# Steps of a context stream placed among 512 row gathers by the length of their products

## The reference, cut to what matters

```
def _peer(h, w_q, sub_keys, u_tab, v_tab):          # first block
    qry = (t @ w_q) ...;  scores = einsum("thpd,hpkd->thpk", qry, sub_keys)
    s_top, i_top = top_k(scores, 16);  ...;  best, pos = top_k(cand, 16)
    gate = softmax(best)
    u = u_tab[ib];  act = gelu(einsum("td,thkd->thk", tb, u))
    vv = v_tab[ib];  return einsum("thk,thkd->td", gb * act, vv)

# second block, layer 0, the context's part
hc = modulate(rmsnorm(ctx));  ctx = ctx + cg1 * pool_mixer(hc)
ctx = ctx + cg2 * conv_ffn(modulate(rmsnorm(ctx)))   # 1024 -> 2 x 2816 -> 1024, width-3 conv
# layer 1: hc = modulate(rmsnorm(ctx)); keys and values of attention from hc
```

## Time and profile before

| | us |
|---|---|
| median of 3 runs | 1712.83 (1711.22 to 1714.83) |
| the profiled execution, its own time | 1713.59 |
| its span, first to last instruction | 1711.7 |
| first gather issued | 326.9 |
| last gather issued | 1125.3 |

### The profile page before, as it was taken

One profiled execution on the slowest core, in us unless ns is written; L12 is line 12 of the kernel. 1 busy time (PEld: TensorE's weight loads), 2 busy tenths in 40 slices (PEclk: granted clock), 3 DMA queues, 4 the chain that ended last, 5 costly groups with the idle time before them and its releaser, 6 DMA issues.

```text
span 1711.7 us, 23479 instructions
## 1 busy us (share of the span) xinstructions
PE 1498.0 (88%) x9034; PEld 1109.4 (65%) x9034; DVE 1093.5 (64%) x2121; ACT 554.4 (32%) x782; POOL 790.4 (46%) x746
## 2 busy tenths in 40 slices
PE   7999998775566699999788866989999999999999
PEld 6997676663212266666333432449999985699999
DVE  4865654689489867766856665237775436567753
ACT  6652121211221131322100011236654524466542
POOL 0024230276667765746777777624561101225630
PEclk9999999997878899999999997999999898999999
DMA  7447770498999999999999999985654425746550
GB/s 273 149 148 294 278 278 25 158 398 305 384 398 400 409 396 391 394 382 400 406 404 400 404 371 408 408 307 187 195 185 158 175 105 191 266 130 196 192 178 26
DMA packets 188575, 477.24 MB, mean 279 GB/s; under 512 B 10544, under 2 KB 80432, under 8 KB 185264
## 3 DMA queue, kind: packets, MB, share of 16 engines
q0 software_dynamic: 73728, 268.47, 40.3%
q1 hardware_dynamic: 114736, 207.27, 34.1%
HBM read 474.65 MB, written 1.05 MB: 278 GB/s over the span
## 4 chain that ended last, share of the span: by engine, by line
PE 57%; DMA 15%; DVE 10%; POOL 7%; issue 4%; ACT 1%; DVEq 0%; ACTq 0%; SPq 0%; POOLq 0%
PE ps L666 57%; DMA arena<-in_peer_v,cl 8%; POOL arena L2723 6%; DMA wring<-in_ffn_w_up 3%; DVE arena L1802 2%; DMA wring<-in_peer_v,cl 2%; DVE arena L1419 1%; POOL wring L2723 1%; DMA arena<-in_peer_u,arena 1%; PE ps L670 1%; DVE arena L1425 1%; DMA wring<-in_peer_u,arena 1%; DVE wring L1802 1%; DVE arena L1732 0%; DMA wring<-in_ada 0%
## 5 line engine op out<-in xcount | busy, mean ns | idle before, releaser
L666 PE MATMUL ps<-arena,wring 128*128 128x256 f32 (+2 forms) x2360 | 595.5, 489 | 105.5 <-DMA arena<-in_peer_v,cl 97.4
L666 PEld LDWEIGHTS ps<-arena,wring 128*128 128x128 f32 (+1 forms) x2360 | 330.4, 167 | 352.7 <-DMA arena<-in_peer_v,cl 176.5
L1802 DVE CUSTOM_DVE_ANT_0 arena<-arena 128x1024 f32<-128x1024 f32 x214 | 257.2, 1227 | 124.7 <-DMA arena<-in_peer_u,arena 121.3
L2723 POOL DMA_INDIRECT arena<-in_peer_u,arena x214 | 240.2, 1123 | 198.5 <-DVE arena L1760 80.0
L2723 POOL DMA_INDIRECT arena<-in_peer_v,cl x214 | 222.9, 1042 | 82.4 <-issue 57.9
L2130 ACT ACT_TABLE_LOAD x64 | 82.1, 1283 | 388.1 <-DVE arena L1802 266.9
L1419 DVE TENSOR_TENSOR wl<-wring,wh 128x2048 fp32r<-128x2048 f32 (+1 forms) x76 | 167.8, 2208 | 60.7 <-ACT wh L2133 58.6
L666 PE MATMUL ps<-hh,wh 128*128 128x256 f32 x704 | 201.2, 286 | 3.9 <-DVE hl L1425 3.9
L666 PE MATMUL ps<-hl,wh 128*128 128x256 f32 x704 | 200.8, 285 | 0.0
L666 PE MATMUL ps<-hh,wl 128*128 128x256 f32 x704 | 200.7, 285 | 0.0
L1425 DVE SCALAR_TENSOR_TENSOR cvb<-ps,vec,cvb 128x255 f32<-128x255 f32 x264 | 127.5, 483 | 106.9 <-ACT cvb L2130 99.6
(11 more groups left out here) (261 smaller groups left out, 2324.0 us busy)
## 6 DMA issues: line engine op xcount, KB each, us to landing
wring<-in_ffn_w_up SPq DMA_DIRECT2D x66, 1024.0 KB, 8.3
wring<-in_ada SPq DMA_DIRECT2D x24, 2048.0 KB, 8.7
wring<-in_ffn_w_down SPq DMA_DIRECT2D x12, 2048.0 KB, 8.4
wring<-in_w_in SPq DMA_DIRECT2D x8, 2048.0 KB, 8.1
wring<-in_ffn_w_down SPq DMA_DIRECT2D x6, 1536.0 KB, 7.9
wring<-in_peer_wq SPq DMA_DIRECT2D x4, 2048.0 KB, 20.7
wring<-in_attn_w_qkv SPq DMA_DIRECT2D x4, 2048.0 KB, 9.0
wring<-in_w_out SPq DMA_DIRECT2D x2, 2048.0 KB, 8.2
```

Of the source, the lines that this page charges most:

```text
L666: return pe.matmul(o, l, r, start=start, stop=stop)
L1802: ve.tensor_tensor_reduce(out=o, in0=o, in1=h2[:, t, :], scale=1.0, scalar=0.0, op0=MUL, op1=ADD, accum_out=dots[j % 2][:, k:k + 1]).then_ ...
L2723: po.indirect_dma_start(out=ring[n % NR], out_offset=None, in_=table, in_offset=bass.IndirectOffsetOnAxis(ap=which, axis=0)).then_inc(S[f" ...
```

## The change

`woven` no longer compares with an even threshold. It keeps `due`, the rest at which the next step is taken, first 4, and after step k adds `rests(k)`: 4 up to step 9; then 7 after a query product and 2 after its scores up to step 15; 2 for the short and empty steps, but 4 after steps 23 to 26; 10 after each up product (34 to 55); 5 after each down step (58 to 81); 4 from step 89. All three engines use it. The steps' contents, the gathers and the loads' order are the same. The steps stand at these rests, worked out from both rules:

| step | before | after |
|---|---|---|
| 0 to 10 | 4 to 44 | 4 to 44 |
| 12, 14, 15 | 55, 66, 72 | 53, 62, 69 |
| 16 | 77 | 71 |
| 18, 20 | 88, 100 | 75, 79 |
| 22, 26 | 111, 133 | 83, 97 |
| 34 | 178 | 115 |
| 55 | 296 | 325 |
| 58 | 312 | 339 |
| 81 | 441 | 454 |
| 89, 91 | 486, 497 | 473, 481 |

```diff
+    def rests(k):
+
+
+        if k < 10:
+            return 4
+        if k < 16:
+            return 2 if k % 2 else 7
+        return 4 if 23 <= k < 27 or k >= 89 else 10 if 34 <= k < 56 else 5 if 58 <= k < 82 else 2
+
     def woven(peer, context):
 
 
-        n, steps, half = 0, 0, None
+        n, steps, half, due = 0, 0, None, 4
         for what in peer:
             if what == "rest":
                 n += 1
                 if n == half:
                     next(context, None)
                     half = None
-                elif n >= (4 * (steps + 1) if steps < 11 else 44 + 56 * (steps - 10) // 10):
+                elif n >= due:
+                    due += rests(steps)
                     steps += 1
                     if next(context, None) == "half":
                         half = n + 3
```

## The result

The changed kernel took 1718.57 us in the median of 20 runs against 1714.84 us for the kernel before in as many; the ratio is 1.0023 with an interval of 1.0014 to 1.0032. A repetition with 12 runs gave 1716.08 us and a ratio of 1.0004 (0.9992 to 1.0016). So it is no faster: +0.23% or 3.7 us in the first comparison, whose interval leaves out zero, and +0.04% in the second, whose interval includes it. The forecast was +1.5 us.

What follows compares the result with a forecast made beforehand. The prediction took DMA and TensorE as equally full, so relieving TensorE wins nothing; 0 + 1 - 0.5 + 1 + 0 = +1.5 us, 1713.59 to 1715.1, median 1714.3 us. Range 1711 to 1718, wide range 1706 to 1724.

Steps and rivals of the forecast that it cites:

- both resources were full: Stage of the gathers, at the up products: TensorE and DMA each need 10.1 us per product; relieving one leaves the other.
- Queries: Rests 44 to 75, sixth and seventh heads' products taken earlier: 0 us, bounds -1 and +4.
- First norm: First norm and pooling, steps 16 to 33, denser: VectorE stands 15 us, mostly covered by loads; +1 us, between 0 and 9.
- Up products: Steps 34 to 55, every 10 rests instead of 5.6: DMA alone bounds, a pause near 750 goes; -0.5 us, bounds -9 and 0.
- Down products: Steps 58 to 81, every 5 rests instead of 5.6: TensorE at 95%, last rests without room; +1 us, bounds 0 and +4.
- TensorE freed: Up products: TensorE was the bound and the even load frees it, -9 us, giving 1704 us; chance 0.2, wholly or in part.
- Cover fails: First norm: loads issued at 431 land before about 460, DMA is out of work 9 us, giving 1722 us; chance 0.2.
- Down steps or clock: Dense down steps or the clock make TensorE late, +5 us, giving 1718 us; chance 0.1.

Runs made afterwards that it cites:

- half bytes: Half of each load of the context's up weights left out; ratio to before 0.9897 in the kernel before, 0.9862 in the changed kernel.
- half products: Half of each context up product left out, loads kept; ratio to before 0.9993 in the kernel before, 0.9997 in the changed kernel.
- early loads: Late constants, pooling weights and first up weights asked for before the wait for last scores; ratio to before 0.9972 (kernel before), 0.9973 (changed kernel).

## Why the prediction was right

**That both resources were full, and that the transfers decide.** Right, and now shown: half of TensorE's products took nothing off (798.4 to 798.5 us). What carried it in the prediction was the packet time per megabyte, 2.57 against 2.55 us. That the two bounds were equal, at 10.1 us each, was wrong by some 5%: TensorE needs less, as the half bytes show. It had no weight in the sum, since the change relieves TensorE alone.

**Queries, 0 us.** The share from 380 to 440 went from 0.90 to 0.89, 0.6 us. Right.

**First norm, +1 within 0 to 9.** Most of the timing held: root ready at 453.4 (said 452.8, with a first gather 2.5 us later in this profile), gather 68 at 447.1 (446), gather 74 at 458.9 (458), a stand of 16.2 us (15), though in two parts and from 432.4 on (437). The backlog lasted longer than said: the share is 1.04 from 460 to 520, and the pause came from 520 to 540, where it reads 0.90, 20 x (1 - 0.90/1.035) = 2.6 us. The term was undersized by 1.6 us. The prediction named 460 to 520 as the place to look. What it left out is what refills an empty queue. GpSimd's issues in that pause:

```profile
522.42 1.76 POOL L2733 DMA_INDIRECT arena<-in_peer_u,arena  x1 [0.31 <-issue]
524.49 1.99 POOL L2733 DMA_INDIRECT arena<-in_peer_u,arena  x1 [0.30 <-issue]
```

From 519.1 to 549.6 it issues 22 gathers one behind the other, never idle for more than 0.31 us, so it waits for no row. That is 1.45 us each, with single ones of 1.8 to 2.0 us, where the transfer of a row takes 1.28. Before, it issued 14 gathers between 520 and 540, as many as now, and the share was 1.03. So the difference lies in the backlog: once that is spent, GpSimd can't soon build it up again.

**Up products, -0.5 us.** The share stayed at 1.04 from 590 to 722 and from 740 to 810. TensorE's busy share was said to fall to some 80% and reads 88%: 115.5 of 132 us. The products aren't the reason, they take 0.229 us an instruction (60.6 us for 265) where it was 0.231. It is the value rows' instructions, from 590 to 722, before and after:

```profile
L666 PE MATMUL ps<-arena,wring 128*32 128x512 f32 x136 | 28.7, 598 | 0.0
```

```profile
L676 PE MATMUL ps<-arena,wring 128*32 128x512 f32 x135 | 46.7, 634 | 14.0 <-DMA arena<-in_peer_v,cl 14.0
```

They are busy 0.346 us each in place of 0.211, in a stretch where TensorE now waits for rows; why isn't settled. The prediction took 0.24 for them, and the difference is some 14 of the 132 us. It had no weight in the sum. The granted clock cost nothing visible: it was 0.95 to 0.97, and with half products even 0.87 cost nothing.

**Down products, +1 us.** Wrong in sign. From 920 to 1020 the share rose from 1.01 to 1.03 (405 GB/s for 388), 2 us less pause. With the new weave the down loads are issued from 791 to 952 us, before it was 772 to 922, so they are still there when the denser TensorE work comes; the prediction weighed TensorE's 95% and not that these loads move along with the steps. That they are the cause is argued, no run isolated it. The repetition reads 1.03 too, and the kernel with only the norms moved, whose down steps lie 6.7 rests apart, reads 1.01 as before.

**The sum.** +1 - 0.5 + 1 said; +2.6, -0.5, -2 and some 0.6 found, near 0.7 us, against a stage of -0.5 us in the first profile and +1.2 in the second. Two errors of 1.6 and 3 us cancel, and that is luck (the second is uncertain by about 1 us, since the shares are rounded). Totals of +0.23 and +0.04% with +1.5 us (0.09%) forecast lie on both sides. The median of 1718.57 us is within the wide range of 1706 to 1724 and just over the forecast's own, 1711 to 1718. What the first comparison's 3.7 us hold, beyond the forecast's 1.5, stays open: the stages in the profiles don't show it, and no experiment isolated such a part.

**The rivals.** TensorE freed: excluded by the half products. Cover fails: not in the changed kernel, whose share was 1.04 from 460 to 520. With half the bytes and with early loads it does fail, at 8.7 us from 440 to 560 in both, near the 9 us that the prediction gave without a working. Down steps or clock: its price of 1718 us is the nearest to the first total, but from 920 to 1020 the share is 1.03 with TensorE at 87%, so it isn't the reason.

## What to carry to other kernels

An engine that is busy 100% of a stretch isn't yet its bound: compare what the other full resource does per unit of work, and if both come out near to equal, relief of the one that isn't the bound gives nothing until the other shrinks too. A transfer queue that is full turns any order of the same bytes into the same time, so look for its pauses and ask which loads could be issued earlier to fill them. And a load that is under way during a stall is its cover: moving it to fill one pause can open another.

## What the runs showed of the hardware

Mean share of the 16 DMA engines reads 1.03 to 1.04 when they never pause, and the cost is 2.55 to 2.57 us per MB for gathers of 4 KB rows, with TensorE full or not. GpSimd takes 0.94 us for the issue of a gather of 128 rows and 0.3 us to the next, at times up to 2.0 us, so it can keep up with the transfers' 1.28 us and hardly run ahead of them. A stretch at 0.97 to 1.00, which looks full, has by that measure 3 to 6% of pause. The part behind the last gather, the same instructions in every complete kernel here, took 581.0 to 594.1 us in the profiles: that spread is larger than all that this change does.
